# Half-way products with seven block products: the order of ten jobs per strip pair, and who forms the double sums of weights

## What is computed

```python
x = x + 0.5 * SwiGLU_1(RMSNorm(x))          # (silu(h @ w_gate) * (h @ w_up)) @ w_down
u = RMSNorm(x) @ W_in                       # two groups of attention heads
x = x + concat(groupA_out, groupB_out) @ W_out
x = x + 0.5 * SwiGLU_2(RMSNorm(x))
x = RMSNorm(x)
```

## Time and profile before

| | |
|---|---|
| Time, median of 3 runs | 1810.5 us (1809.49 to 1810.59) |
| Profiled execution, its own time | 1810.47 us |
| Span of that execution in the profile | 1808.7 us |
| TensorE busy in the span | 1790.4 us (99%), 8236 products |
| VectorE, ScalarE, GpSimd busy | 1433.5, 994.5, 94.1 us |
| Mean granted clock of TensorE | 0.997 of full |

### The profile page before, as it was taken

How to read it: one execution, slowest core, us unless ns; L and a number is a source line. 1 busy time by engine, 2 the same in 40 slices (tenths; PEclk the granted TensorE clock), 3 DMA queues, 4 the chain that set the end, 5 groups by cost and what they waited for, 6 DMA issues and landing times.

```text
span 1808.7 us, 21462 instructions
## 1 busy us (share of the span) xinstructions
PE 1790.4 (99%) x8236; PEld 1487.8 (82%) x8236; DVE 1433.5 (79%) x1719; ACT 994.5 (55%) x1232; POOL 94.1 (5%) x79
## 2 busy tenths in 40 slices
PE   9999999999999999999999999999999999999998
PEld 7888788887888888888888888888788887888887
DVE  7889888899888877656666567889888887668875
ACT  7555455556445636565656455555455555345554
POOL 0100000100000000100000000000000110000000
PEclk9999999999999999999999999999999999999999
DMA  9888658886688858655465466787658887578863
GB/s 322 246 254 244 210 199 230 251 252 196 212 243 246 263 177 255 208 167 175 150 198 162 152 230 224 233 254 235 215 196 229 257 250 232 201 230 248 259 199 114
DMA packets 251093, 398.74 MB, mean 220 GB/s; under 512 B 18160, under 2 KB 96752, under 8 KB 250992
## 3 DMA queue, kind: packets, MB, share of 16 engines
q1 hardware_dynamic: 233760, 364.44, 59.6%
q0 software_dynamic: 16320, 31.46, 10.8%
q10 hardware_dynamic: 912, 1.48, 0.2%
HBM read 378.31 MB, written 2.10 MB: 210 GB/s over the span
## 4 chain that ended last, share of the span: by engine, by line
PE 92%; DVE 6%; ACT 1%; DMA 1%; issue 0%; ACTq 0%; DVEq 0%; POOL 0%; SPq 0%
PE psum L2021 56%; PE psum L2075 17%; PE psum L1934 7%; PE psum L2036 6%; PE psum L1939 3%; DVE w_split L1335 2%; PE psum L2056 1%; ACT w_split L835 1%; DMA w_raw<-in_ffn_up 0%; DVE strip_sum L1390 0%; DVE squares L1380 0%; DVE h_planes L1431 0%; DVE head_out L1436 0%; DVE pair_sums L1326 0%; DVE squares L1366 0%
## 5 line engine op out<-in xcount | busy, mean ns | idle before, releaser
L835 ACT ACTIVATE w_split<-w_raw 128x1024 fp32r<-128x1024 f32 (+2 forms) x560 | 551.0, 1001 | 475.2 <-PE psum L2021 270.4
L1335 DVE TENSOR_TENSOR w_split<-w_raw,w_split 128x1024 fp32r<-128x1024 f32 (+2 forms) x560 | 622.8, 1149 | 108.0 <-ACT w_split L835 103.3
L2021 PE MATMUL psum<-w_split,x_split 128*128 128x512 f32 x2832 | 655.9, 390 | 0.4 <-DVE w_split L1335 0.4
L2021 PEld LDWEIGHTS psum<-w_split,x_split 128*128 128x128 f32 x2832 | 529.2, 188 | 113.7 <-DVE w_split L1335 4.1
L2021 PE MATMUL psum<-w_split,h_planes 128*128 128x512 f32 x1920 | 441.2, 391 | 6.8 <-DVE w_split L1335 4.9
L2021 PEld LDWEIGHTS psum<-w_split,h_planes 128*128 128x128 f32 x1920 | 360.8, 188 | 84.0 <-DVE w_split L1335 6.6
L1185 DVE TENSOR_TENSOR w_split<-w_raw,w_split 128x1024 fp32r<-128x1024 f32 (+1 forms) x244 | 283.9, 1190 | 95.7 <-ACT w_split L719 94.1
L719 ACT ACTIVATE w_split<-w_raw 128x1024 fp32r<-128x1024 f32 (+1 forms) x244 | 246.5, 1032 | 204.8 <-PE psum L2021 148.2
L2075 PE MATMUL psum<-w_split,pair_sums 128*128 128x512 f32 x624 | 162.5, 389 | 0.0
L2075 PE MATMUL psum<-w_split,x_split 128*128 128x512 f32 x540 | 142.2, 390 | 0.0
L2075 PEld LDWEIGHTS psum<-w_split,pair_sums 128*128 128x128 f32 x624 | 117.1, 188 | 24.3
(11 more groups left out here) (247 smaller groups left out, 1213.2 us busy)
## 6 DMA issues: line engine op xcount, KB each, us to landing
w_raw<-in_ffn_down SPq DMA_DIRECT2D x64, 1024.0 KB, 6.3
w_raw<-in_ffn_up SPq DMA_DIRECT2D x47, 1024.0 KB, 5.7
w_raw<-in_ffn_gate SPq DMA_DIRECT2D x46, 1024.0 KB, 7.4
w_raw<-in_ffn_gate SPq DMA_DIRECT2D x82, 512.0 KB, 4.2
w_raw<-in_ffn_up SPq DMA_DIRECT2D x80, 512.0 KB, 5.2
w_raw<-in_ffn_up POOLq DMA_DIRECT2D x60, 512.0 KB, 6.2
w_raw<-in_w_in SPq DMA_DIRECT2D x48, 512.0 KB, 4.6
w_raw<-in_w_in SPq DMA_DIRECT2D x24, 1024.0 KB, 5.2
```

Source lines behind the costliest of these rows:

```text
L835: nc.scalar.activation(w_split[:, split_at(c), 0, part[0]:part[1]], w[:, part[0]:part[1]], ACT.Copy).then_inc(hi_made, 1)
L1335: nc.vector.tensor_tensor(w_split[:, split_at(c), 1, part], w[:, part], w_split[:, split_at(c), 0, part].bitcast(F32), ALU.subtract).then_ ...
L2021: ins = mm(psum[:, bank + t, :], x[:, a, t * P:(t + 1) * P], w[:, b, k, :], start=kk == from_ and (a, b) == (0, 0) and t in begins, stop=k ...
```

## The change

Of the two raw chunks whose blocks are used twice, the second is no longer chunk 3 but chunk 4, and a plain job stands behind each blocks job. The list is now J0, J1 plain, J2 blocks, J3 plain, J4 blocks, J5 plain, J6 and J7 sums, J8 and J9 plain. The step of L1347 is dropped; in its place GpSimd issues an accumulating transfer for each of the two chunks as soon as VectorE has made the low part of its blocks job (`add_wide_blocks`). The remaining two steps of VectorE stand at n=3 (first chunk, behind the low part of J5) and n=4 (second chunk, behind the low part of J6); before, they stood at n=1 and n=2 for w=0 and n=0 and n=2 for w=1. The results leave PSUM one step later (n=7 and n=8, was n=6 and n=7), `moved_high` and `moved_low` move from n=4 to n=5, and the sums of x for the group that follows (`pair_of_blocks`, twice) move from n=7 and n=8 of w=1 to n=9 of w=0. The places of the raw chunks and the jobs that free them follow.

```diff
-WIDE_JOBS = (("plain", 0), ("plain", 1), ("blocks", 2), ("blocks", 3), ("plain", 4), ("sums", 2), ("sums", 3),
-             ("plain", 5), ("plain", 6), ("plain", 7), ("plain", 8), ("plain", 9))
-WIDE_PAIR_OF = {2: 0, 3: 1}
-WIDE_FREED_BY = (-4, -3, -2, -1, 0, 1, 5, 6)
+WIDE_JOBS = (("plain", 0), ("plain", 1), ("blocks", 2), ("plain", 3), ("blocks", 4), ("plain", 5), ("sums", 2), ("sums", 4),
+             ("plain", 6), ("plain", 7), ("plain", 8), ("plain", 9))
+WIDE_PAIR_OF = {2: 0, 4: 1}
+WIDE_PLACE = (0, 1, 2, 3, 0, 1, 3, 2)
+WIDE_FREED_BY = (-4, -3, -2, -1, 0, 1, 3, 6)
+WIDE_NEXT_PLACES = (1, 0, 3, 2)
+WIDE_SUMMED_BY_TRANSFERS = (0, 1)
+WIDE_SUMS_AT = (3, 4)
...
+            def add_wide_blocks(ph, w):
+
+                source = weights_of(ph)
+                for raw, m in WIDE_PAIR_OF.items():
+                    if m in WIDE_SUMMED_BY_TRANSFERS:
+                        blocks = raw_at(ph, w, raw).rearrange("p (q n) -> p q n", n=2 * STRIP)
+                        pool.wait_ge(lo_made, lo_value(seven_base(ph, w) + WIDE_JOBS.index(("blocks", raw))))
+                        nc.gpsimd.dma_start(blocks[:, 0:4:2, :], source(2 * w + 1, 0)[:, 2 * m:2 * m + 2, :],
+                                            accum_op=ALU.add).then_inc(wide_block_sums[m], 16)
...
                 if by_transfer(ph, m):
-                    dve.wait_ge(block_sums[m], 16 * (group_count(ph, i) + 1))
+                    dve.wait_ge(*transfer_done(ph, i, m))
...
+                        if n == 8:
+                            dve.wait_ge(chunk_used, used_value(base + 8))
+                            dve.wait_ge(wide_step, done + per_group - 4)
+                            for t, addend in enumerate((p1, u3)):
+                                scaled_add(left[:, t, :], t, addend if ph["first"] else left[:, t, :])
+                            dve.wait_ge(wide_step, done + per_group - 2)
+                            dve.sem_inc(psum_freed, 2)
                         seven_low(ph, w, n + 2, ph["kn"])
-                        if n in (1 - w, 2):
-                            sum_blocks(ph, w, n // 2)
-                        if n == 4 and w == 0:
+                        if n in WIDE_SUMS_AT:
+                            sum_blocks(ph, w, WIDE_SUMS_AT.index(n))
+                        if n == 5 and w == 0:
                             moved_low(ph["groups"] - 1, ph["g0"] + ph["groups"] - 1)
-                        if n == 6:
-                            dve.wait_ge(chunk_used, used_value(base + 6))
+                        if n == 7:
+                            dve.wait_ge(chunk_used, used_value(base + 7))
...
+                        if n == 9 and w == 0:
+                            dve.wait_ge(hidden_32, ph["last_moved"])
+                            for m in range(2):
+                                pair_of_blocks(ph["build"] + 2 + m, ph["x_norm"], m, 1)
```

More of the change, by code:

```diff
@@ L94, in hybrid_layer @@
     s = g = r = part_at = moved_at = extra = sevens = builds = wide_steps = gates = sums = 0
+    wide_sums_steps = sum(2 if m in WIDE_SUMMED_BY_TRANSFERS else 3 for m in range(2))
     group_sums_steps = sum(2 if m in SUMMED_BY_TRANSFERS else 3 for m in range(3))
@@ L137, in plan_ffn @@
                     extra, sevens, builds, wide_steps = extra + 4, sevens + 2, builds + 4, wide_steps + 2 * (8 if part == 0 else 12)
-                    sums += 12
+                    sums += 2 * wide_sums_steps
+                    phases[-1]["places"] = [places]
+                    for _ in range(2):
+                        places = [places[k] for k in WIDE_NEXT_PLACES]
+                        phases[-1]["places"].append(places)
                 if turns:
@@ L315, in hybrid_layer @@
         block_sums = [sem(f"block_sums{n}") for n in range(3)]
+        wide_block_sums = [sem(f"wide_block_sums{n}") for n in range(2)]
         weight_sums = sem("weight_sums")
@@ L420, in hybrid_layer @@
         blocks_value = lambda ph, i, m: 16 * ((group_count if m == 2 else seven_count)(ph, i) + 1)
-        by_transfer = lambda ph, m: in_group(ph) and m in SUMMED_BY_TRANSFERS
+        by_transfer = lambda ph, m: m in (SUMMED_BY_TRANSFERS if in_group(ph) else WIDE_SUMMED_BY_TRANSFERS)
+        transfer_done = lambda ph, i, m: ((block_sums[m], 16 * (group_count(ph, i) + 1)) if in_group(ph) else
+                                          (wide_block_sums[m], 16 * (ph["sevens"] + i - ph["gates_done"] + 1)))
         sum_steps = lambda ph, m: 2 if by_transfer(ph, m) else 3
         sums_before = lambda ph, k, m: (GROUP_SUMS_AT[k], k) < (GROUP_SUMS_AT[m], m) if in_group(ph) else k < m
-        weight_sums_value = lambda ph, i, m: (ph["sums"] + (i - ph["plain"]) * (group_sums_steps if in_group(ph) else 6) +
+        weight_sums_value = lambda ph, i, m: (ph["sums"] + (i - ph["plain"]) * (group_sums_steps if in_group(ph) else wide_sums_steps) +
                                               sum(sum_steps(ph, k) for k in ((0, 1, 2) if in_group(ph) else (0, 1)) if sums_before(ph, k, m)))
@@ L430, in raw_at @@
             else:
-                at = ph["places"][0][raw % 4]
+                at = ph["places"][i][WIDE_PLACE[raw]] if raw < 8 else ph["places"][i + 1][raw - 8]
             return w_raw[:, at, :]
@@ L508, in wide_pair_chunks @@
                     for j in range(8):
-                        sp.wait_ge(lo_made, lo_value(seven_base(ph, i) + (-6 if j == 0 and i else WIDE_FREED_BY[j])))
+                        sp.wait_ge(lo_made, lo_value(seven_base(ph, i) + (-5 if j == 0 and i else WIDE_FREED_BY[j])))
                         dst = raw_at(ph, i, j).rearrange("p (k n) -> p k n", n=2 * STRIP)
@@ L679, in add_all_blocks @@
                             add_blocks(ph, i)
+                    if ph["kind"] == "seven_wide":
+                        for w in range(2):
+                            add_wide_blocks(ph, w)
             norm_rstd(0)
@@ L1528, in seven_wide @@
                                     nc.vector.tensor_tensor(out, out, addend, ALU.add).then_inc(wide_step, 1)
-                        if n == 7:
-                            dve.wait_ge(chunk_used, used_value(base + 7))
-                            dve.wait_ge(wide_step, done + per_group - 4)
-                            for t, addend in enumerate((p1, u3)):
-                                scaled_add(left[:, t, :], t, addend if ph["first"] else left[:, t, :])
-                            dve.wait_ge(wide_step, done + per_group - 2)
-                            dve.sem_inc(psum_freed, 2)
-                        if w and n == 7:
-                            dve.wait_ge(hidden_32, ph["last_moved"])
-                            pair_of_blocks(ph["build"] + 2, ph["x_norm"], 0, 1)
                         if w and n > 7:
                             pair_low(ph["build"] + n - 6, n - 8, 1)
-                        if w and n == 8:
-                            pair_of_blocks(ph["build"] + 3, ph["x_norm"], 1, 1)
+                        if n == 9 and w == 0:
+                            dve.wait_ge(hidden_32, ph["last_moved"])
+                            for m in range(2):
+                                pair_of_blocks(ph["build"] + 2 + m, ph["x_norm"], m, 1)
             def group_x_lo(ph, i):
@@ L2102, in seven_wide @@
                             continue
-                        m = raw - 2
+                        m = WIDE_PAIR_OF[raw]
                         k = WIDE_PAIRS[m]
```

15 lines of the change are left out of this document (8 added, 7 removed).

## The result

| | before | after |
|---|---|---|
| Median of 15 runs each, us | 1810.17 (1809.23 to 1810.59) | 1813.86 (1812.70 to 1815.82) |
| Ratio, 95% interval | | 1.0021 (1.0014 to 1.0029) |
| Profiled execution, own time / span | 1810.47 / 1808.7 | 1814.08 / 1812.3 |
| VectorE busy | 1433.5 | 1419.7 |

The forecast was 1813.3 us with a range of 1811.4 to 1815.3. The measured 1813.9 lies in it. The whole interval of the ratio lies above one, and its middle stands just past the 0.2% that I called the edge of what can be told.

The account below looks back on a forecast made before the run. The prediction took TensorE, busy for 99% of the span, as the bound, so only its pauses count. The terms -5.9 + 6.2 + 2.2 + 0.3 = +2.8 us on 1810.5 gave 1813.3 us, range 1811.4 to 1815.3.

Parts of the forecast that it names:

- The pauses that go (-5.9): TensorE's pause before J4 at w=0 vanishes in each of three phases, 1.96 us each with the restart: -5.9 us.
- J7 (+6.2): TensorE waits 0.85 us before J7, 1.03 with restart, behind the late sums' chain; six times, +6.2 us.
- J8 (+2.2): At w=0 moved_low delays J8's low part; TensorE waits 0.56 us, 0.74 with restart, three times: +2.2 us.
- what a pause costs beyond itself: Restart of TensorE's products behind a pause, reckoned at 0.18 us from 24 products taking 5.78 us, not 5.60.
- J10 (+0.3): Second phase: additions between J9's and J10's low parts make TensorE wait about 0.1 us, 0.3 with restart, once.
- The transfers (0): Twelve GpSimd transfers replacing L1347 land in time, 5.8 to 7.9 us against 9.5 and 10 of room: no cost.
- Rival 3: A transfer lands late, sharing engines with other loads; at 11 us, +9 us, 1822 us; chance 0.04.
- The clock (no fall): TensorE's clock stays full in all three phases, despite smaller pauses, 0.85 and 0.56 us, twice as many.
- rival 2: Clock falls at w=0 between the J7 and J8 pauses, 1.7 us three times, 5.1; 1818.4 us; chance 0.06.
- Rival 1: J7 does not wait, its chain being 0.85 us shorter; TensorE has no pause there; 1804.6 us; chance 0.05.

Follow-up runs that it names:

- No pause: New job order, all sums on VectorE at n=2 and n=3, hidden columns at n=4, two second-phase additions behind J10's low part; 1804.44 us, ratio to before 0.9967.
- moved_n4: Changed kernel with moved_high and moved_low at n=4 instead of n=5; 1810.85 us, ratio to before 1.0005.
- sums_n3_n3: Changed kernel with the second sums of weights at n=3, right behind the first, instead of n=4; 1805.79 us, ratio to before 0.9978.
- sums_on_vector: Changed kernel without its transfers, all sums on VectorE, still at n=3 and n=4; 1832.78 us, ratio to before 1.0123.
- late_transfers: Changed kernel with each of the twelve transfers issued one job later; 1835.33 us, ratio to before 1.0138.
- transfers_alone: Kernel before, its own job order, with only the change's transfers added and the remaining sums at n=2 and n=3; 1822.43 us, ratio to before 1.0069.
- sums_n2_n3: Changed kernel with its transfers, sums at n=2 and n=3 instead of n=3 and n=4; 1806.63 us, ratio to before 0.9981.

## Why the prediction was right, point by point

- **The pauses that go (-5.9).** All three went. "No pause" against before is 1.99, 1.95 and 1.97 us per phase, 5.91 together.
- **J7 (+6.2).** Reckoned 0.85 us, six times; measured 0.87, six times. `moved_n4`, where they stand alone, gives 6.3 us for all six (its three phases less "no pause"). `sums_n3_n3` removes them by moving the second sums, `sums_on_vector` lengthens them by what it adds to the chain. This term is shown.
- **J8 (+2.2).** Reckoned 0.56, three times; measured 0.55. `moved_n4` removes them and shows that the place of the hidden columns was the cause. They cost 0.67 each (first phase 88.85 against 88.19, third 86.61 against 85.93), 2.0 together: what a pause costs beyond itself was 0.12 here and not 0.18.
- **J10 (+0.3).** The pause is 0.44 us and not 0.1. TensorE wanted J10 when I had said, 15.7 us after the start of J7's low part. It came at 16.14 and not at 15.8: the additions took 0.2 more than the rows of before gave, and from the low part to the product it was 1.37 and not 1.27 us. The place was right; the size, a small difference of two sums of 16 us, was short by 0.3. It cost some 0.5 us (1.13 that `moved_n4` saves in the second phase, less 0.67 for J8).
- **The transfers (0).** Nobody waited for the line L694. It landed after 5.9 to 6.7 us, its room was 9.3 (issue at 186.6, L1376 at 195.91). Rival 3 stood for the right danger: `late_transfers` and `transfers_alone` show waits for transfers where the room is smaller.
- **The clock (no fall).** It was 1.00 in all three phases; rival 2 did not come. (The prediction calls the pauses twice as many as before. They are ten against three.) The Trainium skill ("TensorE: Matmul & The Clock Gate", "A second HAM failure mode: psum-queue depth-cycling") lets the clock swing where short idle times between groups of products are frequent. Pauses of 0.87 and 0.55 us within 4 us were not enough for it here. Nor were 1.02, 1.95 and 0.51 us within 9 us in `transfers_alone`; behind pauses of 3.2 us in `sums_on_vector` the clock fell four times out of six.
- **Rival 1 (no wait at J7)** would have needed a chain 0.85 us shorter; it was 0.02 longer.

So the sum measured in the three phases is -5.9 + 6.3 + 2.0 + 0.5, +2.85 us before rounding, for the +2.8 reckoned; J8's and J10's errors cancel. So the forecast's +2.8 is met by the right pauses, with some luck in two of their sizes. The last 0.8 us of the measured difference is not of these terms. In the profiled execution most of it lies in two waits of TensorE outside these phases, one before 16.9 us and one of 0.35 us at 409.7, in an input phase. The edit is at neither place. `late_transfers` waits 0.27 us at the same product as at 409.7, the other eight kernels have no pause of 0.2 us there. Whether it is scatter from one execution to the next or an effect of earlier transfers on later ones stays open.

## What to carry to other kernels

Work taken from an engine pays only where that engine is what others wait for; read this from the wait before each job, not from busy time. Where one engine must write something that a second rounds and the first then uses, the distances between the engines (here 1.46 and 1.09 us) weigh as much as the operations, and two such rounds in a row are dearer than both pieces of work placed side by side: one step of a loop was worth 8 us here. And when two edits come together, price each without the other; here one of them alone did the work.

## What was not expected of the hardware

**A fall of the clock that costs almost nothing.** In the last down phase, kernel before, TensorE pauses 1.95 us at 1524.86 and then runs at 1.2 GHz for a while the earlier trace rows. In the changed kernel there is the same pause, and no fall. Timeline, all engines, changed kernel:

```profile
1528.58 5.74 PE L2046 MATMUL psum<-w_split,h_planes 128*128 128x512 f32 x24 [1.94 <-DVE w_split L1211]
...
1533.27 1.06 ACT L832 ACTIVATE h_planes<-lo_sum 128x1024 fp32r<-128x1024 f32 x1 [3.16 <-DMA lo_sum<-head_out]
...
1534.36 1.23 DVE L1457 TENSOR_TENSOR h_planes<-lo_sum,h_planes 128x1024 fp32r<-128x1024 f32 x1 [2.43 <-ACT h_planes L832]
...
1535.73 5.46 PE L2046 MATMUL psum<-w_split,h_planes 128*128 128x512 f32 x23 [1.42 <-DVE h_planes L1457]
```

And VectorE before:

```profile
1530.34 1.23 DVE L1431 TENSOR_TENSOR h_planes<-lo_sum,h_planes 128x1024 fp32r<-128x1024 f32 x1 [2.13 <-ACT h_planes L806]
```

24 products in 5.74 us is full speed (at 0.227 us each and 0.39 for the last they take 5.60; the rest is the restart). But then TensorE waits 1.42 us for hidden columns whose transfer lands at about 1533.3. From the first of the 24 products to the 25th it is 7.15 us in both kernels, to 0.01. In the changed kernel the transfer sets the end: VectorE starts 5.78 us behind the first product, TensorE 1.37 us behind VectorE. Before, VectorE starts 5.48 us behind it, so TensorE could have gone on at 6.85, and the slow products lasted until 7.15. In the prediction I had priced the fall at 1.7 us from these very rows. That is what the products lost; the kernel lost some 0.3 us there (an estimate, from the two times just given). Over all ten kernels, the stretch from product 6900 to 7000 took 26.47 to 26.77 us in the eight with a fall, and 26.43 and 26.57 in the two without (`sums_n2_n3` and the change). Clock losses, too, have to be weighed against what waits behind them.

**Pauses and the clock.** Over all runs: behind 0.87 and 0.55 us together, and behind 1.78 us, it stayed at 1.00. The other cases are mixed. (All lengths here but the idle time of 1.95 us at 1524.86 are distances between starts less the usual 0.227; that one is 2.11 by this measure.)

| pause before, us | clock full behind it | clock fell behind it |
|---|---|---|
| 1.02, 1.95 and 0.51 within 9 us | `transfers_alone`, w=0, first phase; the other two are alike | |
| 1.09 and 1.96 within 5 us | | `late_transfers`, third phase |
| 2.10 or 2.11, last down phase | the change, `sums_n2_n3` | the other eight |
| 2.15 and 2.28 | `late_transfers`, w=1, phases one and two | |
| 3.2 | two of six, `sums_on_vector` | four of six |
| 3.9 to 5.1 | | `late_transfers`, w=0, three phases |

The length of the pause alone doesn't decide.

**Accumulating transfers are dear on the DMA engines.** The queues of the changed kernel: packets, MB, share of 16 engines' span.

```profile
q1 hardware_dynamic: 233760, 364.44, 59.6%
q0 software_dynamic: 19584, 37.75, 13.0%
```

Per MB the queue that holds them takes 0.34% of the engines' time (13.0 / 37.75), the plain loads 0.16% (59.6 / 364.44): a little over twice. The queue q0 holds nothing but accumulating transfers (72 of 512 KB in the change). In the kernel before it had 31.46 MB and 10.8%, so the twelve more add 2.2% for 6.3 MB, the same 0.35% per MB. That they cost no time in the three phases of the change follows from the waits: every pause of TensorE there is of the chain above, and ScalarE (L861) waits for no load of `in_ffn_down`.
